# Rotary halves of the retention heads swapped by four 32-partition SBUF-to-SBUF DMAs instead of a permutation product

## The reference, cut to what matters

```python
def rope(x, pos):
    half = x.shape[-1] // 2
    inv = ROPE_BASE ** (-jnp.arange(half, dtype=jnp.float32) / half)
    ang = pos.astype(jnp.float32)[:, None] * inv[None, :]
    cos = jnp.cos(ang)[None, :, None, :]
    sin = jnp.sin(ang)[None, :, None, :]
    xf = x.astype(jnp.float32)
    x1, x2 = xf[..., :half], xf[..., half:]
    return jnp.concatenate([x1 * cos - x2 * sin, x1 * sin + x2 * cos], axis=-1).astype(x.dtype)

rq, rk = rope(rq, pos), rope(rk, pos) * (RET_DK ** -0.5)
```

## Time and profile before

| | us |
|---|---|
| median of 3 runs | 1182.33 |
| lowest, highest | 1181.81, 1182.85 |
| the profiled execution's own time | 1181.68 |
| its span, first to last instruction | 1179.9 |
| TensorE busy in the span | 1139.1 (97%) |
| ScalarE, VectorE, GpSimd busy | 584.9, 534.0, 762.1 |
| mean granted TensorE clock | 0.995 |

### The profile page before, as it was taken

How to read it: one execution, slowest core, us unless ns; L and a number is a source line. 1 busy time by engine, 2 the same in 40 slices (tenths; PEclk the granted TensorE clock), 3 DMA queues, 4 the chain that set the end, 5 groups by cost and what they waited for, 6 DMA issues and landing times.

```text
span 1179.9 us, 24430 instructions
## 1 busy us (share of the span) xinstructions
PE 1139.1 (97%) x8620; PEld 1095.5 (93%) x8620; DVE 534.0 (45%) x1068; ACT 584.9 (50%) x1036; POOL 762.1 (65%) x592
## 2 busy tenths in 40 slices
PE   5999999999999999999999999999999999999995
PEld 4897899999999999999989878999999999999995
DVE  5346233243866551255152642424367665315523
ACT  5564354445346663344456644555443666524431
POOL 3664555656876777777676555565577677777772
PEclk9999999999999999999999999999999999999998
DMA  7754545545544455455566555554444454554551
GB/s 276 255 189 164 193 134 179 160 132 170 164 144 144 145 147 156 144 152 153 151 217 209 171 213 172 164 156 137 141 146 143 144 156 145 148 155 142 150 160 45
DMA packets 53211, 190.77 MB, mean 162 GB/s; under 512 B 6033, under 2 KB 7313, under 8 KB 52881
## 3 DMA queue, kind: packets, MB, share of 16 engines
q1 hardware_dynamic: 43632, 159.15, 44.2%
q10 hardware_dynamic: 9504, 30.56, 7.0%
HBM read 181.15 MB, written 8.53 MB: 161 GB/s over the span
## 4 chain that ended last, share of the span: by engine, by line
PE 90%; DVE 5%; issue 1%; ACT 1%; DMA 1%; POOL 0%; DVEq 0%; SPq 0%; ACTq 0%; POOLq 0%
PE bank L1067 46%; PE bank L1098 30%; PE bank L1112 5%; PE bank L1117 1%; DMA raw<-w 1%; PE bank L1323 1%; DVE arena L695 1%; DVE arena L785 1%; PE bank L1314 1%; PE bank L1200 1%; PE bank L1189 1%; PE bank L1218 1%; PE bank L1333 1%; PE bank L1303 1%; ACT whi L290 1%
## 5 line engine op out<-in xcount | busy, mean ns | idle before, releaser
L255 POOL TENSOR_TENSOR wlo<-raw,whi 128x512 fp32r<-128x512 f32 x588 | 761.9, 1317 | 398.4 <-PE bank L1098 191.9
L290 ACT ACTIVATE whi<-raw 128x1024 fp32r<-128x1024 f32 x294 | 310.9, 1058 | 284.1 <-PE bank L1067 168.4
L1098 PE MATMUL bank<-oh,whi 128*128 128x320 f32 x848 | 267.3, 315 | 3.5 <-DVE arena L961 2.1
L1098 PE MATMUL bank<-oh,wlo 128*128 128x320 f32 x848 | 262.0, 309 | 0.0
L1098 PE MATMUL bank<-ol,whi 128*128 128x320 f32 x848 | 261.9, 309 | 0.0
L1067 PE MATMUL bank<-hh,whi 128*128 128x320 f32 x832 | 257.6, 310 | 0.0
L1067 PE MATMUL bank<-hl,whi 128*128 128x320 f32 x832 | 257.1, 309 | 0.0
L1067 PE MATMUL bank<-hh,wlo 128*128 128x320 f32 x832 | 257.1, 309 | 0.0
L1098 PEld LDWEIGHTS bank<-oh,whi 128*128 128x128 f32 x848 | 159.2, 188 | 11.6 <-issue 5.5
L1098 PEld LDWEIGHTS bank<-ol,whi 128*128 128x128 f32 x848 | 159.3, 188 | 0.3
L1098 PEld LDWEIGHTS bank<-oh,wlo 128*128 128x128 f32 x848 | 159.2, 188 | 0.0
(11 more groups left out here) (193 smaller groups left out, 1321.3 us busy)
## 6 DMA issues: line engine op xcount, KB each, us to landing
raw<-w SPq DMA_DIRECT2D x296, 512.0 KB, 3.6
arena<-cache_k ACTq DMA_DIRECT2D x16, 512.0 KB, 6.2
arena<-cache_v ACTq DMA_DIRECT2D x16, 512.0 KB, 5.1
arena<-st_in ACTq DMA_DIRECT2D x8, 512.0 KB, 4.7
sst_out<-arena ACTq DMA_DIRECT2D x8, 512.0 KB, 4.2
con<-consts SPq DMA_DIRECT2D x1, 1284.0 KB, 13.5
x<-x_in SPq DMA_DIRECT2D x2, 640.0 KB, 10.4
arena<-mem_in SPq DMA_DIRECT2D x2, 512.0 KB, 6.4
```

Of the source, the lines that this page charges most:

```text
L255: i = pool.tensor_tensor(out=wlo[:, s % 2, h], in0=raw[:, s, h], in1=whi[:, s, h].bitcast(f32), op=ALU.subtract)
L290: nc.scalar.activation(whi[:, s, :], raw[:, s, :], ACT.Copy).then_inc(hi_ready, 1)
L1098: r = MM(o, a, b[:, k, 0:n], start=k == 0 and i == 0, stop=k == KT_ - 1 and i == 2, skip_group_check=True)
```

## The change

The permutation matrix and the matrix beside it that nothing uses leave the constants, so that the first constant load falls from 256 KB to 128 KB. The sign of the swap moves into the sine table. `rot` and its four calls leave TensorE's list, with the semaphore `rot_used`. ACT gets `swap_halves(r)`, called behind each of the last four `qk`: it waits until its own copy is in SBUF, then issues four DMAs that each bring 32 partitions of 1280 bytes to `turned[:, r]`. `rope(r)` waits for these DMAs, multiplies `turned` by the sine in place, with both operands in SBUF, and links that product to the next instruction by a wait; the cosine product, the sum and the rest stay.

```diff
-                def rot(r):
-                    buf = (kd if r < 2 else qd)[:, 2 + r % 2, :]
-                    pe.wait_ge(evac, lv * EVACS + 5 + 4 + r + 1)
-                    if r:
-                        pe.wait_ge(rot_used, lv * 4 + r)
-                    else:
-                        pe.wait_ge(b_ready, lv * 2 + 1)
-                    MM(C[0][:, 0:T], perm, buf, start=True, stop=True).then_inc(rot_done, 1)
...
+                def swap_halves(r):
+
+                    buf = (kd if r < 2 else qd)[:, 2 + r % 2, :]
+                    act.wait_ge(evac, lv * EVACS + 5 + 4 + r + 1)
+                    for r0 in range(0, P, 32):
+                        act.dma_start(turned[r0:r0 + 32, r, :], buf[r0 ^ 32:(r0 ^ 32) + 32, :]).then_inc(rot_done[r], 16)
...
                 qk(4, kd[:, 2, :])
+                swap_halves(0)
                 qk(5, kd[:, 3, :])
+                swap_halves(1)
                 xhi(0)
                 xhi(1)
                 xturn(2)
                 xturn(3)
                 qk(6, qd[:, 2, :])
+                swap_halves(2)
                 for b in range(4):
                     load_v(b)
                 xexp_(4)
                 qk(7, qd[:, 3, :])
+                swap_halves(3)
                 xhi(2)
                 xhi(3)
...
-                    dve.wait_ge(rot_done, lv * 4 + r + 1)
-                    V.tensor_tensor(out=rt[:, 0, :], in0=C[0][:, 0:T], in1=con[:, K_SIN:K_SIN + T], op=ALU.mult).then_inc(rot_used, 1)
+                    dve.wait_ge(rot_done[r], lv * 64 + 64)
+                    link(V.tensor_tensor(out=turned[:, r, :], in0=turned[:, r, :], in1=con[:, K_SIN:K_SIN + T], op=ALU.mult))
                     link(V.tensor_tensor(out=rt[:, 1, :], in0=buf[:, p, :], in1=con[:, K_COS:K_COS + T], op=ALU.mult))
-                    link(V.tensor_tensor(out=rt[:, 0, :], in0=rt[:, 0, :], in1=rt[:, 1, :], op=ALU.add))
+                    link(V.tensor_tensor(out=rt[:, 0, :], in0=turned[:, r, :], in1=rt[:, 1, :], op=ALU.add))
...
-    c[:, K_SIN:K_SIN + T] = np.sin(ang)
+    c[:, K_SIN:K_SIN + T] = np.where(r[:, None] % DK < DK // 2, -1.0, 1.0) * np.sin(ang)
```

More of the change, by code:

```diff
@@ L42 @@
 NPAR = C_CS + FT * 16
-K_ID, K_ONE, K_CEN, K_PERM, K_MASK, K_COS, K_SIN = 0, 128, 256, 384, 512, 832, 1152
-K_DQ, K_DK, K_RST, K_DE, K_BM, NCON = 1472, 2112, 2752, 3072, 3076, 3080
+K_ID, K_ONE, K_MASK, K_COS, K_SIN = 0, 128, 256, 576, 896
+K_DQ, K_DK, K_RST, K_DE, K_BM, NCON = 1216, 1856, 2496, 2816, 2820, 2824
 def build_trunk(nc, w, x_in, mem_in, cache_k, cache_v, st_in, consts, final_g,
@@ L136, in build_trunk @@
         rt = at(o_gn + 2 * T, 2, T)
+        turned = at(o_s + 2848, 4, T)
         on, gsq = at(o_gn, 2, 3 * P), at(o_ke, 2, 3 * P)
@@ L157, in build_trunk @@
         tb = at(o_g + 3500, 2, T)
-        ident, ones, cent, perm = (con[:, k:k + P] for k in (K_ID, K_ONE, K_CEN, K_PERM))
+        ident, ones = (con[:, k:k + P] for k in (K_ID, K_ONE))
         pb = [ctx.enter_context(nc.psum_tensor(f"bank{i}", [P, 512], f32)) for i in range(8)]
@@ L199, in build_trunk @@
         z_done, ln_ready, b_ready, eb_ready = sem("z_done"), sem("ln_ready"), sem("cumsum_ready"), sem("decays_ready")
-        rot_done, rot_used, ke_ready, qd_ready = sem("rot_done"), sem("rot_used"), sem("kend_ready"), sem("qdkd_ready")
+        ke_ready, qd_ready = sem("kend_ready"), sem("qdkd_ready")
+        rot_done = [sem(f"rotated{i}") for i in range(4)]
         vh_ready = sem("sample_values_halves")
@@ L1236, in _ @@
                 unit(U_QK + 6, oh, ol, T)
-                rot(0)
                 unit(U_QK + 7, oh, ol, T)
@@ L1240, in _ @@
                 pv(3)
-                rot(1)
                 toks = (0, P, T - P)
@@ L1250, in _ @@
                 sample_values(0)
-                rot(2)
                 vunit(U_GV + 3, 3, oh, ol, B[0:3])
-                rot(3)
                 pe.wait_ge(evac, lv * EVACS + 13)
@@ L1272, in _ @@
                 pe.wait_ge(xos, lv + 1)
-                pe.wait_ge(rot_used, lv * 4 + 4)
                 for a in range(2):
@@ L1434 @@
 EVACS = 37
-PER = {"act": 6, "dve": 198}
+PER = {"act": 6, "dve": 202}
 def constants():
@@ L1443, in constants @@
     c[:, K_ONE:K_ONE + P] = 1.0
[L1444 to L1449, removed]
     for a in range(2):
```

## The result

The changed kernel takes 1188.94 us (median of 5 runs, 1188.74 to 1190.05) against 1182.54 for the kernel before: a ratio of 1.0056, 95% interval 1.0044 to 1.0067. It is slower by 6.4 us. I had forecast 1181.8, no change, in a range up to 1185.6: the forecast was wrong. The span of the profiled execution went from 1179.9 to 1187.2 us, 7.3 longer.

What follows compares the result with a forecast made beforehand. TensorE, busy 97% of the span, was taken as the bound. Per layer, +0.83 us for a later start and -1.10 for removed products gave -0.27; two layers, -0.54, took 1182.33 to 1181.8 us, range 1178.8 to 1185.6.

Steps and rivals of the forecast that it cites:

- the price of an issue: On ACT, each added DMA issue was priced at 0.445 us, from four load_v issues taking 1.78 us.
- 0.59 as upper bound: Highest price allowed for an ACT issue, in us, from the idle one group of issues left before the exponential.
- the forecast 112.23: Layer 0: TensorE starts the value unit behind its wait at 112.23 us, 0.83 later than 111.40.
- rival 2: TensorE's clock falls in the longer wait before the value unit, making the kernel slower than before; chance 0.14.
- rival 2's two sums: Whole-kernel times with the unit behind the wait losing 1.9 us a layer (1185.6) or 3.8 (1189.4).
- my own wait of 3.2: TensorE's forecast idle before the value unit, from 109.01 to 112.23 us, instead of 1.3.
- Rival 1: Cheap issues on ACT: at 0.27 us or less each, TensorE starts early and the kernel is faster; chance 0.23.
- the products behind the wait: rot(2) and rot(3) on TensorE: removing them was to gain 2 x 0.55 = 1.10 us a layer in full.
- a forecast of 101.0: On DVE, rope(0) was to run from about 101.0 us, no longer waiting for TensorE until 104.34.
- the 0.64 MB of traffic: Other DMA traffic per layer, at hours when queues are half idle; forecast to cost nothing.
- The floor of 110.85: DVE's normalisation, held until POOL's subtractions end, was to keep TensorE from starting the value unit before 110.85 us.
- rival 1's first case: Issues at 0.27 us or less: TensorE starts at 110.85, gaining 1.65 us a layer, 3.3 in all, 1179.0 us.

Runs made afterwards that it cites:

- e4: The changed kernel with each swap DMA reading 32 rows of the cosine table from HBM, result not computed; 1185.68 us, ratio 1.0027.
- e5: The kernel before with the sixteen DMAs a layer added and waited for, TensorE's permutation products kept; 1191.58 us, ratio 1.0080.
- e6: The changed kernel without the sixteen DMAs a layer, VectorE multiplying the tile itself by the sine, result not computed; 1176.95 us, ratio 0.9956.
- e3: The changed kernel with one DMA of 128 partitions per swap instead of four of 32, halves not exchanged; 1178.16 us, ratio 0.9963.
- e1: The changed kernel with the last two swaps issued behind xhi(3) instead of ahead of load_v and xhi(2); 1176.81 us, ratio 0.9958.
- e2: The changed kernel with eight unused products added on TensorE behind pv(3), to fill its wait; 1186.52 us, ratio 1.0040.
- e8: e4 with five unused products added on TensorE behind pv(3), result not computed; 1182.44 us, ratio 1.0004 to the kernel before.
- e10: The changed kernel with only swap_halves(2) issued behind xhi(3), swap_halves(3) staying ahead of xhi(2); 1180.97 us, ratio 0.9990.
- e9: The changed kernel with only swap_halves(3) issued behind xhi(3), swap_halves(2) staying ahead of load_v; 1184.32 us, ratio 1.0018.

## Why the prediction was wrong, point by point

The step that failed first is the price of an issue: "take 0.445, the price of four in a row", with 0.59 as upper bound. It measured 0.61 in the median and up to 0.65, and the rows of four took 2.44 to 2.67 us. The 0.59 bounded nothing: it was the idle of ScalarE before the exponential, not the length of an issue. All rows that I had were loads and stores with HBM on one side and 128 rows; I noted that bytes and rows differ, and not that the source does, which is what e4 shows to matter. By the same formula the start moves from the forecast 112.23 by 0.66 (swap 2), 0.36 (load_v, which I held fixed), 0.89 (swap 3) and the early 0.24 to 114.4; it was 114.22. The path from the issues to TensorE's start was right, its terms too small by 1.9 us in layer 0 and by 1.7 in layer 1.

The second is the clock. The sum put it at nothing. It was rival 2, with a chance of 0.14, and it is not a rival to the forecast but belongs to it: with issues near my 0.445 the clock fell in both layers of e4. In the changed kernel it cost 1.81 + 2.42 = 4.2 us. That rival 2's two sums, 1185.6 and 1189.4, lie so near to e4's 1185.68 and the changed kernel's 1188.94 is luck: the first has 3.8 us for the clock where e4 lost 1.61 + 1.42 = 3.0, the second has 7.6 where 4.2 were lost and the dearer issues made up the rest. I took the wait after which the clock is known to stay (1.31) and the one after which it is known to fall (some 4) and put the decision near the upper end, though my own wait of 3.2 lay nearer to that end. It fell with a wait of 2.3 already. The page "TensorE: Matmul & The Clock Gate" of the Trainium skill, section Part 1, has an idle engine fall to half clock, and the windows after agree: 0.50 behind an idle stretch. The range reached only to one of the two losses, never to dear issues and a fallen clock together, though the first makes the second likelier.

Rival 1 lost. The rule of the Trainium skill's page "DMA: Bandwidth & Descriptors" that it names, that initiating a DMA is usually small beside the DMA itself, agrees with the trace (0.61 beside a landing of 3.3) and says nothing of what counts here, since issues were on the path and landings weren't.

Right were: 1.1 us a layer from the products behind the wait (the step of 1.01 is 133.48 - 133.03 = 0.45 now, and e5 less the changed kernel is 2.6 for two layers); rope(0) at 101.16 for a forecast of 101.0; that landings and the 0.64 MB of traffic are hidden (e6); that the other swaps and the moved load_v cost nothing; and VectorE's L797 (now L810) as what ends the wait. The floor of 110.85 set by VectorE was met in e3 (110.65), but it isn't a floor: I had xlo(2) wait until GpSimd's pair ends, and in e1 the normalisation, which rope(0) no longer holds up, began at 107.28 and xlo(2) at 109.24, a microsecond before the pair ended at 110.23. TensorE started at 109.72. So rival 1's first case had too small a gain.

## What to carry to other kernels

A DMA issued by a compute engine costs that engine's list its issue time, here 0.44 to 0.65 us a piece: count what stands behind each issue, and put issues behind the last instruction that somebody on the critical path waits for. With the same sixteen DMAs a layer, and the same work off TensorE, the change cost 6.4 us with the issues in one place and gained 5.3 with eight of them in another. And when an edit lengthens an idle stretch of TensorE, price the clock with it: a wait of 2.3 to 5 us cost another 1.4 to 2.6 us in the unit behind it.

## What the runs showed of the hardware that I had not expected

An issue from ScalarE takes 0.61 us when four with the source in SBUF follow one another and 0.44 when the source is HBM, with the same 32 rows; a single one with SBUF as source and 128 rows takes 0.47, a single one from HBM 0.33. The first load_v behind a row of SBUF sources takes 0.59, behind e4's row of HBM sources 0.43. Now and then one issue takes far longer than its neighbours (1.82 in e2, 1.52 in e1, 1.36 in e8); no run shows why.

TensorE's clock stayed at 1.00 over waits of 1.31, 1.50 and, behind the added products, 1.72 and 1.94 us; it fell with waits of 2.27, 3.08, 3.47, 4.01 and 4.97 (layer 0 of e10, e9, e4, e5 and the changed kernel). In some it was still full at the first matmuls behind the wait and fell only then, and the length of the wait doesn't sort them: after 3.77 us (e5, layer 1) four matmuls ran at full clock, after 3.33 (e4, layer 1) not even the first. The loss in the unit was 1.4 to 1.6 us for waits of 2.3 to 3.8, and 2.6, 2.4 and 1.8 for those of 4.01, 4.75 and 4.97.
